# Moving the split weight tiles by some tens of bytes against the moving tiles

## The reference

```python
h = h + swiglu(rmsnorm(h, ffn_norm[layer]), ffn_w_gate_up[layer], ffn_w_down[layer])
def swiglu(h, w_gate_up, w_down):
    g, u = jnp.split(h @ w_gate_up, 2, axis=-1)
    return (jax.nn.silu(g) * u) @ w_down
def sq_relu_mlp(h, w1, w2):
    return jnp.square(jax.nn.relu(h @ w1)) @ w2
```

## Time and profile before

| | |
|---|---|
| median of 3 runs | 2628.09 us (2623.52 to 2632.59) |
| span of the profiled execution | 2627.9 us |
| TensorE busy (products) | 2557.7 us, 97% |
| TensorE weight loads | 2102.4 us, 80% |
| VectorE / ScalarE / GpSimd busy | 1581.3 / 1048.3 / 258.4 us |
| granted TensorE clock, mean | 0.990 |

### The profile page before, as it was taken

One profiled execution on the slowest core, in us unless ns is written; L12 is line 12 of the kernel. 1 busy time (PEld: TensorE's weight loads), 2 busy tenths in 40 slices (PEclk: granted clock), 3 DMA queues, 4 the chain that ended last, 5 costly groups with the idle time before them and its releaser, 6 DMA issues.

```text
span 2627.9 us, 37789 instructions
## 1 busy us (share of the span) xinstructions
PE 2557.7 (97%) x13070; PEld 2102.4 (80%) x13070; DVE 1581.3 (60%) x2460; ACT 1048.3 (40%) x1663; POOL 258.4 (10%) x187
## 2 busy tenths in 40 slices
PE   8999999999999999999989999999999999999997
PEld 6887788888877778888878776788888888888886
DVE  6764665656578866565665786655555665644445
ACT  5334522223347852222353266553223522522333
POOL 2320100000320010000030100310000301300002
PEclk9999999999999999999999999999999999999999
DMA  3221344444320034444432100234444243332222
GB/s 133 73 88 65 118 137 144 144 145 151 135 73 25 26 113 144 144 144 144 144 121 73 41 1 1 81 112 144 144 149 140 96 144 116 104 100 96 96 96 80
DMA packets 79337, 277.46 MB, mean 106 GB/s; under 512 B 8448, under 2 KB 11904, under 8 KB 78720
## 3 DMA queue, kind: packets, MB, share of 16 engines
q1 hardware_dynamic: 58560, 205.55, 23.6%
q10 hardware_dynamic: 20672, 70.51, 8.1%
HBM read 273.92 MB, written 2.10 MB: 105 GB/s over the span
## 4 chain that ended last, share of the span: by engine, by line
PE 85%; DVE 8%; ACT 3%; issue 2%; DMA 1%; POOL 1%; ACTq 0%; DVEq 0%; SPq 0%; POOLq 0%
PE banks L2425 64%; PE banks L2566 5%; PE banks L3002 2%; PE banks L2469 2%; DVE w_lo L1403 1%; PE banks L2944 1%; PE banks L2600 1%; PE banks L2876 1%; DMA w_raw<-weights 1%; PE banks L2853 1%; PE banks L2956 1%; ACT w_hi L679 1%; PE banks L2973 1%; DVE nsa_e L1968 1%; PE banks L2838 1%
## 5 line engine op out<-in xcount | busy, mean ns | idle before, releaser
L679 ACT ACTIVATE w_hi<-w_raw 128x1024 fp32r<-128x1024 f32 x367 | 386.4, 1053 | 621.5 <-PE banks L2425 514.9
L2425 PE MATMUL banks<-h_hi,w_hi 128*128 128x512 f32 x1600 | 628.2, 393 | 1.1 <-DVE w_lo L1403 0.7
L2425 PE MATMUL banks<-h_hi,w_lo 128*128 128x512 f32 x1600 | 623.4, 390 | 0.0
L2425 PE MATMUL banks<-h_lo,w_hi 128*128 128x512 f32 x1600 | 623.2, 389 | 0.0
L1403 DVE TENSOR_TENSOR w_lo<-w_raw,w_hi 128x1024 fp32r<-128x1024 f32 x367 | 474.2, 1292 | 108.7 <-ACT w_hi L679 92.1
L2425 PE MATMUL banks<-g_hi,w_hi 128*128 128x512 f32 (+1 forms) x1108 | 427.7, 386 | 9.8 <-DVE w_lo L1403 8.8
L2425 PE MATMUL banks<-g_lo,w_hi 128*128 128x512 f32 (+1 forms) x1108 | 423.9, 383 | 0.0
L2425 PE MATMUL banks<-g_hi,w_lo 128*128 128x512 f32 (+1 forms) x1108 | 423.7, 382 | 0.0
L2425 PEld LDWEIGHTS banks<-h_hi,w_hi 128*128 128x128 f32 x1600 | 300.5, 188 | 66.5 <-issue 2.8
L2425 PEld LDWEIGHTS banks<-h_lo,w_hi 128*128 128x128 f32 x1600 | 300.6, 188 | 62.8 <-issue 1.7
L2425 PEld LDWEIGHTS banks<-h_hi,w_lo 128*128 128x128 f32 x1600 | 300.4, 188 | 62.9
(11 more groups left out here) (411 smaller groups left out, 3290.8 us busy)
## 6 DMA issues: line engine op xcount, KB each, us to landing
w_raw<-weights SPq DMA_DIRECT2D x384, 512.0 KB, 3.3
ada_raw<-ada ACTq DMA_DIRECT2D x112, 512.0 KB, 3.3
nsa_bias<-nsa_bias ACTq DMA_DIRECT2D x6, 512.0 KB, 3.4
x<-x SPq DMA_DIRECT2D x4, 512.0 KB, 6.6
out<-x SPq DMA_DIRECT2D x8, 256.0 KB, 2.1
mix_cum<-ret_tab ACTq DMA_DIRECT2D x1, 1024.0 KB, 4.7
rows_c<-c_rows ACTq DMA_DIRECT2D x1, 1024.0 KB, 5.6
nsa_w<-cmp_w ACTq DMA_DIRECT2D x1, 1024.0 KB, 5.4
```

The source lines that it names most:

```text
L679: act.activation(w_hi[s][:], w_raw[s][:], ACT.Copy).then_inc(w_hi_done, 1)
L2425: mm = pe.matmul(bank, w[s][:, k, :], m[:, k, :], start=(n == 0 and a == 0), stop=(n == kts - 1 and a == 2))
```

## The change

The split tiles of slots 0 and 1 get gaps before them, so that they begin at 160 and 224 modulo 512: 32 and 96 bytes past the moving tiles' place (128). The cursor is then brought back to 128 modulo 512, so everything behind them moves up by 512 bytes and keeps its place modulo 512. Slots 2 and 3 are laid down one by one below `ROW_SCALE_AT`, at 320 and 96 modulo 512: 192 and 480 bytes past. `w_hi` and `w_lo` of a slot have the same place. No instruction is added, removed or moved.

```diff
-        w_hi = [sb(f"w_hi{s}", [P, KT, P], F32R) for s in range(2)]
-        w_lo = [sb(f"w_lo{s}", [P, KT, P], F32R) for s in range(2)]
+        w_hi, w_lo = [], []
+        for s, start in enumerate((160, 224)):
+            cursor[0] += (start - cursor[0]) % 512
+            w_hi.append(sb(f"w_hi{s}", [P, KT, P], F32R))
+            w_lo.append(sb(f"w_lo{s}", [P, KT, P], F32R))
+        cursor[0] += (H_AT - cursor[0]) % 512
...
-        W4, _ = place("more_", ROW_SCALE_AT - 4 * 4 * D, [(f"w_{part}{s}", [P, KT, P], F32R) for s in (2, 3)
-                                                          for part in ("hi", "lo")])
-        w_hi += [W4["w_hi2"], W4["w_hi3"]]
-        w_lo += [W4["w_lo2"], W4["w_lo3"]]
+        more_at = ROW_SCALE_AT
+        for s, start in ((3, 96), (2, 320)):
+            more_at -= 2 * 4 * D
+            more_at -= (more_at - start) % 512
+            made, _ = place("more_", more_at, [(f"w_{part}{s}", [P, KT, P], F32R) for part in ("hi", "lo")])
+            w_hi.insert(2, made[f"w_hi{s}"])
+            w_lo.insert(2, made[f"w_lo{s}"])
```

## The result

The changed kernel takes 2680.97 us (4 runs, 2678.2 to 2688.26) against 2630.34 us of the kernel before in the same session: ratio 1.0201, 95% interval 1.0181 to 1.0220. The forecast was 2603.

The account below looks back on a forecast made before the run. TensorE's product stream was taken as the bound, count times pace. From 2627.9 us, 3.1 ns on 8200 products of slots 0 and 1 took 25 us, everything else 0, giving 2603 us; range 2545 to 2650.

Parts of the forecast that it names:

- The bound: Whole kernel: TensorE streams products in 97% of the span, so time is a count of products times their pace.
- That the place matters: Closings: the weight tile's place changes the pace, 120.0 ns on slot 0 against 117.8 on slot 2.
- the mechanism of the prediction: At full clock, weight load and stream read side by side get in each other's way; 13.3 ns per product.
- The step that failed: Slots 0 and 1: new places gain what slot 2's closings show, 2.2 and 6.7 ns, weighted to 3.1 per load.
- The forecast's own place: Slot 2's place, 320 bytes past the moving tiles, from whose closings the gain of 3.1 ns per load was read.
- The term: Slots 0 and 1: 3.1 ns saved on each of 8200 products, 25 us.
- The count: Products of slots 0 and 1 on the path: 8200, so 1 ns per load is worth 8.2 us.
- Slots 2 and 3, the writers, the shifted memory behind the tiles: Slots 2 and 3, between -1.9 and +0.9 us, taken as 0; writers not slowed or hidden; memory behind, 0.
- The ends of the stages: Split, DMA and split on the chain at stage ends: some 17 us in five closings, which don't shrink.
- Rival B: Loops at 512 columns: pace set by something other than place, so no change, 0 ns, 2628 us; chance 0.15.
- Rival C: Slots 0 and 1: the weight tile's own alignment to 64 bytes matters, so slower, +33 us, 2661; chance 0.20.

Follow-up runs that it names:

- the sweep: Small kernel of its own: bursts of 48 fp32r products, the weight tile at each place past the moving tile; 226.7 to 234.2 ns at 512 columns.
- the two half-undone kernels: Changed kernel with slots 0 and 1 back at 0 past: 2628.76 us; changed kernel with slots 2 and 3 back at 320 past: 2680.39 us.

## Why the prediction was wrong, point by point

**The bound** was read rightly: the time is a count of products times a pace, and the chain grew only in the products.

**That the place matters** was right: in the sweep, nothing but the place and the burst before it lies between 226.7 and 234.2 ns, and in the whole kernel the same paces came back. By the rule of the Trainium skill ("SBUF — State Buffer", "Who interferes with whom") that TensorE's reads of the moving operand and of the weights are independent, the place should make no difference; these rows do not agree. That load and stream are what gets in each other's way, the mechanism of the prediction, is not shown. The floor of about 2.5 ns that the Trainium skill gives ("TensorE: Matmul & The Clock Gate", "Wait — 56ns, not 53.3ns?") is not reached by these fp32r products: 13.3 ns over the columns is the least any place had at 512.

**The step that failed** is the one that took "the paces of slot 2, the only other place in the trace" as near rows for the loops: -2.2 and -6.7 ns, weighted to -3.1. They are paces at 256 columns. The bridge was that the excess over the columns at 0 past is 13.3 ns at both widths, "whatever its width"; that was a coincidence read as a law. In the sweep the excess at 0 past is 13.3 ns again at 320 and 384 columns, but 11.7 at 288, 15.0 at 416, 20.0 at 448 and 16.7 at 480. At 320 past the excess is 6.7 or 11.1 ns at 256 columns and 20.0 at 512. The forecast's own place, put under the loops, costs 49 us instead of giving back 25. The support for it, "0 past is the slowest place seen", was true at 256 columns only; at 512 none of the 32 places is faster.

**The term:** instead of -3.1 ns it is +6.6 on slot 0 (233.3 in the rows above) and +7.5 on slot 1 (234.2). In a steady 300 us the count of products fell to 1285 instead of rising to 1345.

**The count** of 8200 products on the path was right: the chain has 7518 of this line and 594 of the first mixer's, before and after. They grew by 49.1 us (1684.8 to 1733.9) and 1.7 us (137.2 to 138.9), and the rest of the chain gave 2.3 back. That is 6.5 and 2.9 ns a product and not the 7.0 of the steady loops. Part of it is that the 240 half-width products of this line gained 1.2 ns (119.7 to 118.5), and that the first product of a short piece takes some 314 ns before and after; in the first mixer, the first piece of 12 also got shorter (4.28 to 2.90 us).

**Slots 2 and 3, the writers, the shifted memory behind the tiles** at nothing: right. 2628.76 and 2680.39 us in the two half-undone kernels answer for slots 2 and 3, 2627.13 us at 256 past for the shift, and VectorE's split takes 1226 ns before and after.

**The ends of the stages** were put at some 17 us on the chain in five closings; the loads of `w_raw` alone take 26.3 us there, in eight pieces. No term of the sum hangs on it.

**Rival B** had the right warning, that no 512-column product stood on another place, but the wrong result. **Rival C** had the sign and two thirds of the size (+33 us, 2661) for a reason that the sweep refutes. The chances gave 0.20 to slower; with a sample at the wrong width that was too little.

## What to carry to other kernels

Where TensorE streams fp32r products back to back with a weight load for each, measure the pace from starts and sweep the weight tile's place against the moving tile's, at the width that the kernel uses: here the choice is worth up to 7.5 ns in 227. Never carry such a pace from one width to another, and read it from bursts that are entered as the kernel enters them. Here, keeping both tiles at the same place modulo 256 was the safe choice: as fast as any at 512 columns, with the same pace whatever came before.

## What the hardware showed that was not expected

- At 512 columns the pace repeats every 256 bytes of relative place. Between a bare burst and the whole kernel it agrees within 0.2 ns (228.9 and 229.1 at 192 past, 233.3 and 233.5 at 320).
- The order of the places turns round with the width. In the sweep's rows at 448 columns, 96 past is faster than 0:

```profile
1151.87 10.06 PE L64 MATMUL banks<-m,w_zero 128*128 128x448 f32 x48
1161.77 9.97 PE L64 MATMUL banks<-m,w_threetwo 128*128 128x448 f32 x48
1171.58 9.77 PE L64 MATMUL banks<-m,w_ninesix 128*128 128x448 f32 x48
1181.19 9.21 PE L64 MATMUL banks<-m,w_zero 128*128 128x416 f32 x48
```

  9.90 / 48 = 206.3 ns at 0 and 9.61 / 48 = 200.2 at 96.
- A pace has a memory: after a change of place the steps differ for four or five products, and some places settle into one of two paces depending on the entry (16 past at 512 columns: 226.7 or 233.4 ns). The entry that helps one place harms another: at 256 columns 320 past holds 117.8 ns behind a burst at 0 and 113.3 after a wait, and 192 past the other way round.
- What collides, load with stream or something else that both use, no run here shows directly.
